# Group means one projection later, a copy ahead of a root, and norm chunks later in two feed-forward tails

## The chip, the cores and the metric

The kernel runs on one NeuronCore of one Trainium2 chip. The time is the device time of one execution in microseconds (us); lower is better. Times of a kernel are given as the median of several executions. A profile is one execution recorded by the hardware profiler; its rows give what each engine did from the start of its span. The engines are PE (TensorE: matmuls; PEld is its weight load), DVE (VectorE), ACT (ScalarE), POOL (GpSimd) and SP (SyncE, which here only issues transfers).

## The reference

One decoder block on a sequence of 1024 tokens of width 1024, in float32:

```python
x = x + 0.5*gt1 * swiglu(modulate(rmsnorm(x, g_ffn1), sh1, sc1), w1, w3, w2)      # feed-forward 1, 2816 wide
h = modulate(rmsnorm(x, g_mix), sh2, sc2)
x = x + gt2 * hybrid_mixer(h, ...)
x = x + 0.5*gt3 * swiglu(modulate(rmsnorm(x, g_ffn2), sh3, sc3), ...)             # feed-forward 2
return modulate(rmsnorm(x, g_final), shf, scf)

# hybrid_mixer, the convolution half (512 channels, 8 groups of 64):
y = gate_b * causal_short_conv(gate_c * u, conv_w)        # three taps
y = rmsnorm(y by group of 64) * conv_norm_g
# the attention half: 4 heads of differential attention; both halves share one output projection
```

The shifts, scales and gates come from a conditioning vector through `w_ada`.

## The kernel before

Everything is held transposed: channels on the 128 partitions, tokens along the free axis, in two halves of 512. Each fp32 operand is split into a high and a low part (`Mh`/`Ml` for the mixer's weights, `Hh`/`Hl` for its input, `Wh`/`Wl` in the feed-forwards), and a product is three matmuls: high by high, high by low, low by high. ACT writes the high part by a copy; DVE subtracts it from the source for the low part. Every engine's instructions are written out by hand in order, and semaphores (`wait_ge`) join them. An instruction that waits holds up all that is behind it on its engine.

**The mixer's convolution half** runs in two groups, `cg` 0 and 1. A group has 12 projections L = 0 to 11, each 24 matmuls of 128x512 into one of six banks: q = L // 3 counts the pairs (tile, half), tile 0 being q 0 and 1, tile 1 being q 2 and 3, and L % 3 chooses u, C or B. The weights of a tile are three units: units 0 to 2 serve L0 to L5, units 3 to 5 serve L6 to L11 (numbers within the first group), so L6 is the first reader of unit 3, L7 of unit 4, L8 of unit 5. PE waits for the low part of a unit (`lo_done`, line 1713) only at even q. After the projections come 16 output tiles t (L = 12 + t), which DVE adds to `X` (`add_out`, line 1256). The group's L0 to L4 run in `project_new`, which takes the input's chunks as they arrive (`h_ready`).

For each q a small chain normalises the tile: DVE multiplies C by u into `CU` (1312), applies the taps (1317, 1321), multiplies by B (1326); ACT squares (794); PE takes the mean over each group of channels (`group_mean(q)`: four small matmuls); ACT takes the root (798 before); DVE inverts and spreads it (1332, 1334); PE broadcasts it (`group_bcast(q)`); DVE scales the tile into `TmpG` (1339); ACT and DVE split that (`g_hi`, `g_lo`). `MEANS[cg]` and `BCASTS[cg]` name the L after which mean and broadcast stand in PE's order.

The splits of the weights stand inside this chain. On ACT, unit 3's high part (`split_hi`, line 709) follows root 0, and unit 4's follows `g_hi` of q 0, hence broadcast 0. On DVE, unit 3's low part (`split_lo`, line 1180) follows the spread of root 0, and unit 4's follows `g_lo` of q 0 and the `CU` of q 1. `copy_u(q)` (781) is ACT's copy of the projection u out of its bank.

**The feed-forward's down part** is seven products of 11 steps g. In the last one (i = 6) PE turns the loop: steps 7 to 10 run for output tile 0, then for tile 1, and so on (`TURNED`). Meanwhile the other half's norm is already applied: DVE's `norm_mul` (1243), ACT's `norm_chunk` (741, two copies in the first feed-forward, one in the second) and, in the first feed-forward only, DVE's `norm_lo` (1249), chunk by chunk. `BEHIND` names which chunk (c0 to c7) and which of the output additions (x0 to x2) stands behind which step g on ACT and DVE. `down_hi` and `down_lo`, which prepare the operands, stand ahead of them in each step. Behind the first feed-forward PE consumes the chunks at once; behind the second they go to the output.

Of the kernel before, what the change touches and what calls it, by code (L numbers as in the profile page):

```python
# [117 lines left out]

TURN = NG - 4
TURNED = [(d, g) for d in (0, 1) for g in (7, 8, 9)] + [(0, 10), (1, 10)] + [(d, g) for d in (2, 3) for g in (7, 8, 9, 10)]  # L120
BEHIND = {6: ("c0",), 7: ("c1", "c2"), 8: ("c3", "c4"), 9: ("c5", "x0"), 10: ("c6", "x1", "c7", "x2")}

X_AFTER = (8, 14, 25, 52)

# [14 lines left out]
    _at += _n  # L139
NCOLS = _at  # L140

MEANS, BCASTS = ((4, 6, 9), (3, 6, 9)), ((5, 7, 10), (4, 7, 10))


def conv_bank(cg, L):
    return (L + (0 if cg else 4)) % BANKS


def program(nc, up_w, down_w, units, ada, x_t, cols_d, lam_d, rope_d, square_d, out_t):
    ctx = ExitStack()  # L150
    with ctx:
# [116 lines left out]
        def half(h):  # L268
            return slice(h * HALF, (h + 1) * HALF)

        def blk(b):
            return slice(b * P, (b + 1) * P)
# [12 lines left out]
        def unit(n):  # L285


            if n < U_Q1:
                return Mh[:, n % RING, :], Ml[:, n % RING, :]
            if n < U_WO + 2:  # L290
                return tuple(m[:, 1 + (n - U_Q1) % 2, :] for m in (Mh, Ml))
            return Wo[:, n - U_WO - 2, 0, :], Wo[:, n - U_WO - 2, 1, :]
# [17 lines left out]
        def sem(name):  # L310
            sems[name] = ctx.enter_context(nc.semaphore(name))
            return sems[name]
# [43 lines left out]
        evac, aevac, ghi, g_ready = sem("evac"), sem("aevac"), sem("ghi"), sem("g_ready")  # L356
# [205 lines left out]
        def _(act):  # L562
# [106 lines left out]
            def down(ph):  # L669
                q = 2 + 4 * ph  # L670
                for m in range(N_DOWN):
# [11 lines left out]
                    if ph == 0 and i == 6 and g in (4, 5, 8):  # L683
                        split_first((4, 5, 8).index(g))
                    for what in BEHIND.get(g, ()) if i == 6 else ():
                        if what[0] == "c":
# [12 lines left out]
            def split_first(n):  # L699

                act.wait_ge(gt_lo, 6 * NG + 2 * n + 2)
                act.wait_ge(raw_loaded[n], 16)
                nc.scalar.activation(Mh[:, n, :], Mr[:, n, :], ACT.Copy).then_inc(hi_done, 1)

            def split_hi(n, wait, value):

                act.wait_ge(wait, value)
                act.wait_ge(raw_loaded[n % RING], 16 * (n // RING + 1))
                nc.scalar.activation(unit(n)[0], Mr[:, n % RING, :], ACT.Copy).then_inc(hi_done, 1)  # L709

            def g_hi(slot, h, wait, value):
                act.wait_ge(wait, value)
                nc.scalar.activation(Gh[:, slot, half(h)], TmpG[:, h, :], ACT.Copy).then_inc(ghi, 1)
# [60 lines left out]
            for cg in range(2):  # L774
                J, E, n0 = JOBS["conv"] + 28 * cg, EVAC["conv"] + 24 * cg, U_CONV + 8 * cg

                def copy_u(q):
                    act.wait_ge(job_done, J + 3 * q + 1)
                    if q >= 2:
                        act.wait_ge(evac, E + 2 * q - 3)  # L780
                    nc.scalar.activation(TmpA[:, q % 2, :], PS[:, conv_bank(cg, 3 * q), :], ACT.Copy).then_inc(aevac, 1)

                if cg:
                    for c in (1, 2):
                        split_hi(n0 + c, job_done, J)
                else:
                    act.wait_ge(hh_done, NH * KT)
                copy_u(0)
                for q in range(4):
                    jt, h, cq = q // 2, q % 2, 4 * cg + q  # L790
                    if h == 1:
                        split_hi(n0 + 3 * jt + 4, job_done, J + 3 * q + 2)
                    act.wait_ge(evac, E + 2 * q + 2)
                    nc.scalar.activation(Sq[:, h, :], CT[:, half(h)], ACT.Square).then_inc(csq_done, 1)
                    if h == 1:
                        split_hi(n0 + 3 * jt + 5, job_done, J + 3 * q + 3)
                    act.wait_ge(cmean_done, cq + 1)
                    nc.scalar.activation(Root[:, 0:8], PS[:, 6, 0:8], ACT.Sqrt, bias=EpsC[:, 0:1])\
                        .then_inc(croot_done, 1)
                    if q < 3:  # L800
                        copy_u(q + 1)
                    if h == 0:
                        split_hi(n0 + 3 * jt + 3, job_done, J + 3 * q + 4)
                    g_hi(jt, h, cg_done, cq + 1)
# [135 lines left out]
        def _(dve):  # L940
# [190 lines left out]
            def down(ph):  # L1131
                q = 2 + 4 * ph
                for m in range(N_DOWN):
# [14 lines left out]
                    if ph == 0 and i == 6 and g in (5, 6, 9):  # L1148
                        split_lo((5, 6, 9).index(g))
                    for what in BEHIND.get(g, ()) if i == 6 else ():  # L1150
                        n = int(what[1])
# [24 lines left out]
            def split_lo(n):  # L1176

                dve.wait_ge(hi_done, n + 1)
                hi, lo = unit(n)
                nc.vector.tensor_tensor(lo, Mr[:, n % RING, :], hi.bitcast(F32), ALU.subtract).then_inc(lo_done, 1)  # L1180
# [260 lines left out]
        def _(pe):  # L1441
            def mm(out, lhs, rhs, first, last):
                return nc.tensor.matmul(out, lhs, rhs, start=first, stop=last)  # L1443
# [160 lines left out]
            def project_new(first, n, h, units):  # L1604


                for k in range(KT + LAG * (units - 1)):
                    for w in range(units):
                        if not w * LAG <= k < KT + w * LAG:
                            continue  # L1610
                        if w == 0:
                            pe.wait_ge(h_ready, KT * h + k + 1)
                        if k == w * LAG:
                            pe.wait_ge(lo_done, n + w + 1)
                            pe.wait_ge(x_added, 28 if h else (24, 24, 25)[w])
                        products(conv_bank(0, first + w), n + w, h, (k - w * LAG,))
                    if h == 0 and k == KT - 1:
                        mean(3)
                    if h == 0 and k == KT + 1:
                        bcast(3)  # L1620
# [59 lines left out]
            for cg in range(2):  # L1680
                J, E, A, G = JOBS["conv"] + 28 * cg, EVAC["conv"] + 24 * cg, AEVAC["conv"] + 4 * cg, GDONE["conv"] + 4 * cg
                n0 = U_CONV + 8 * cg

                def evicted(L):
                    q, w = L // 3, L % 3
                    if L >= 12:
                        return evac, E + 8 + L - 12 + 1
                    return (evac, E + 2 * q + w) if w else (aevac, A + q + 1)

                def group_mean(q):  # L1690
                    pe.wait_ge(csq_done, 4 * cg + q + 1)
                    for b in range(4):
                        made = mm(PS[:, 6, 2 * b:2 * b + 2], Sq[:, q % 2, blk(b)], MeanG[:], True, True)
                    made.then_inc(cmean_done, 1)

                def group_bcast(q):
                    pe.wait_ge(cspread_done, 4 * cg + q + 1)
                    for b in range(4):
                        made = mm(PS[:, 7, blk(b)], Spread[:, q % 2, blk(b)], ident, True, True)
                    made.then_inc(cbc_done, 1)  # L1700

                for L in range(12):
                    q, w = L // 3, L % 3
                    if cg == 0 and L < 5:
                        if w == 0:
                            project_new(L, n0, q, 2 if q else 3)
                    else:
                        if L >= BANKS:
                            pe.wait_ge(*evicted(L - BANKS))
                        elif cg:  # L1710
                            pe.wait_ge(evac, E)
                        if q % 2 == 0:
                            pe.wait_ge(lo_done, n0 + 3 * (q // 2) + w + 1)
                        project(conv_bank(cg, L), n0 + 3 * (q // 2) + w, q % 2)
                    if L in MEANS[cg]:
                        group_mean(MEANS[cg].index(L))
                    if L in BCASTS[cg]:
                        group_bcast(BCASTS[cg].index(L))
                pe.wait_ge(lo_done, n0 + 8)
                for t in range(NH * KT):  # L1720
                    pe.wait_ge(*evicted(12 + t - BANKS))
                    if t % KT == 0:
                        pe.wait_ge(g_ready, G + 3 + t // KT)
                    out_job(conv_bank(cg, 12 + t), (n0 + 6, n0 + 7), [(Gh[:, f, :], Gl[:, f, :]) for f in range(GF)], t)
                    if t == 0:
                        group_mean(3)
                    if t == 3:
                        group_bcast(3)
# [240 lines left out]
```

## Time and profile before

| | |
|---|---|
| median of 3 runs | 1923.37 us (1922.18 to 1923.48) |
| the profiled execution's own time | 1920.22 us |
| its span | 1918.4 us |
| PE busy | 1837.8 us, 96% of the span |
| DVE busy | 1265.1 us, 66% |
| ACT busy | 780.6 us, 41% |
| POOL busy | 262.0 us, 14% |
| chain that ended last | PE 85%, DVE 7%, ACT 4%, issue 2% |

PE's busy share counts its pipelined matmuls as they overlap, so 96% is not PE at its peak. What matters for a change of order are the places where PE stands idle, and what it waits for there: the table of waits and the timeline. A start-to-start distance of about 0.23 us between two 128x512 matmuls is an unhindered PE at full clock. In a timeline row the brackets at the end give the engine's idle time before the instruction and what ended it.

### The profile page before, as it was taken

How to read it: one execution, taken by the hardware profiler on the slowest of the kernel's cores; microseconds unless marked ns; L12 is line 12 of the kernel's file. 1: busy time of each engine (PE TensorE's matmuls, PEld its weight loads, DVE VectorE, ACT ScalarE, POOL GpSimd, SP SyncE). 2: the span in 40 equal slices, each digit the busy share in tenths (PEclk: the TensorE clock that was granted, in tenths of full speed). 3: DMA queues.
4: the chain of work that ended last, by engine and by line, in shares of the span. 5: the costliest groups of instructions: out<-in, count | busy, mean ns of one | idle time of the engine just before them, and what ended most of it. 6: DMA issues, size and time to landing. Idle time of an engine off the chain costs nothing.

```text
span 1918.4 us, 22914 instructions
## 1 busy us (share of the span) xinstructions
PE 1837.8 (96%) x8248; PEld 1471.3 (77%) x8248; DVE 1265.1 (66%) x1946; ACT 780.6 (41%) x1401; POOL 262.0 (14%) x404
## 2 busy tenths in 40 slices
PE   5999999999999999999999999799999999999997
PEld 2778888888788877888876666677888888878885
DVE  5777777777476776434226668787666766567767
ACT  4633333333344555111126565563333333344445
POOL 2021121211210000000303330001111211111000
PEclk9999999999999999999999999899999999999998
DMA  8166565665775312111201110415454554487432
GB/s 314 55 209 218 183 228 187 206 228 176 252 216 158 100 62 76 44 45 44 77 28 39 44 34 1 176 44 198 149 197 154 190 188 149 157 265 218 128 99 88
DMA packets 99984, 269.76 MB, mean 141 GB/s; under 512 B 13088, under 2 KB 13472, under 8 KB 99744
## 3 DMA queue, kind: packets, MB, share of 16 engines
q1 hardware_dynamic: 62064, 146.30, 22.2%
q0 software_dynamic: 34304, 117.46, 18.2%
q10 hardware_dynamic: 3504, 4.53, 1.0%
q8 instruction: 66, 1.08, 0.2%
q14 instruction: 46, 0.38, 0.1%
HBM read 209.53 MB, written 54.53 MB: 138 GB/s over the span
## 4 chain that ended last, share of the span: by engine, by line
PE 85%; DVE 7%; ACT 4%; issue 2%; ACTq 1%; DMA 1%; POOL 0%; DVEq 0%; POOLq 0%
PE PS L1447 60%; PE PS L1443 24%; ACTq L819 1%; PE PS L1848 1%; ACT PR L841 1%; DVE TmpA L1243 0%; DVE NMax L1356 0%; DVE X L1256 0%; DMA X<-x_t 0%; DVE Wl L987 0%; DVE AdaSum L1202 0%; DVE Wl L984 0%; DVE SqSum L1225 0%; DVE CT L1321 0%; ACT Mh L709 0%
## 5 line engine op out<-in xcount | busy, mean ns | idle before, releaser
L1447 PE MATMUL PS<-Bh,Wh 128*128 128x512 f32 x1120 | 442.6, 395 | 5.5 <-ACT T L618 5.5
L1447 PE MATMUL PS<-Bl,Wh 128*128 128x512 f32 x1120 | 441.9, 395 | 0.0
L1447 PE MATMUL PS<-Bh,Wl 128*128 128x512 f32 x1120 | 441.3, 394 | 0.0
L1447 PEld LDWEIGHTS PS<-Bh,Wh 128*128 128x128 f32 x1120 | 210.6, 188 | 57.5 <-DVE Wl L952 6.3
L1447 PEld LDWEIGHTS PS<-Bh,Wl 128*128 128x128 f32 x1120 | 210.5, 188 | 50.3
L1447 PEld LDWEIGHTS PS<-Bl,Wh 128*128 128x128 f32 x1120 | 210.6, 188 | 49.1
L1447 PE MATMUL PS<-Wh 128*128 128x512 f32 x616 | 240.3, 390 | 3.4 <-DVE Wl L987 1.7
L1447 PE MATMUL PS<-Wl,Wh 128*128 128x512 f32 x616 | 239.7, 389 | 0.0
L1447 PE MATMUL PS<-Wh,Wl 128*128 128x512 f32 x616 | 239.7, 389 | 0.0
L984 DVE TENSOR_TENSOR Wl<-RawB,Wh 128x512 fp32r<-128x512 f32 x154 | 106.6, 692 | 136.4 <-ACT Wh L593 135.3
L593 ACT ACTIVATE Wh<-RawB 128x512 fp32r<-128x512 f32 x154 | 97.3, 632 | 230.1 <-PE PS L1447 230.1
L618 ACT ACTIVATE T<-PS 128x512 f32<-128x512 f32 x120 | 71.8, 598 | 265.4 <-PE PS L1447 265.4
L952 DVE TENSOR_TENSOR Wl<-Sums,Wh 128x512 fp32r<-128x512 f32 x160 | 110.3, 690 | 90.5 <-ACT Wh L583 90.3
L1447 PEld LDWEIGHTS PS<-Wh 128*128 128x128 f32 x616 | 115.6, 188 | 28.3 <-DVE T L1018 2.5
L952 DVE TENSOR_TENSOR Wl<-Raw,Wh 128x512 fp32r<-128x512 f32 x136 | 92.9, 689 | 66.0 <-ACT Wh L583 65.8
L1447 PEld LDWEIGHTS PS<-Wh,Wl 128*128 128x128 f32 x616 | 115.6, 188 | 24.2
L1447 PEld LDWEIGHTS PS<-Wl,Wh 128*128 128x128 f32 x616 | 115.6, 188 | 23.8
L1443 PE MATMUL PS<-Hh,Mh 128*128 128x512 f32 x320 | 130.8, 409 | 2.1 <-DVE Hl L1249 1.3
L583 ACT ACTIVATE Wh<-Sums 128x512 fp32r<-128x512 f32 x160 | 98.2, 623 | 79.5 <-DVE Sums L970 54.8
L1443 PE MATMUL PS<-Hl,Mh 128*128 128x512 f32 x320 | 126.5, 395 | 0.0
L1443 PE MATMUL PS<-Hh,Ml 128*128 128x512 f32 x320 | 126.0, 394 | 0.0
L1008 DVE TENSOR_TENSOR T<-T,PS 128x512 f32<-128x512 f32 x120 | 82.3, 686 | 45.9 <-PE PS L1447 43.3
(184 smaller groups left out, 2875.4 us busy)
## 6 DMA issues: line engine op xcount, KB each, us to landing
Raw<-up_w SPq DMA_DIRECT2D x88, 512.0 KB, 5.5
Ada<-ada POOLq DMA_DIRECT2D x72, 512.0 KB, 4.4
g_dram<-T SPq DMA_DIRECT2D x88, 256.0 KB, 2.2
W2s<-down_w POOLq DMA_DIRECT2D x88, 256.0 KB, 4.5
s_dram<-W2s POOLq DMA_DIRECT2D x88, 256.0 KB, 2.5
GQ<-g_dram POOLq DMA_DIRECT2D x88, 256.0 KB, 3.5
RawB<-s_dram SPq DMA_DIRECT2D x88, 256.0 KB, 2.8
RawB<-down_w SPq DMA_DIRECT2D x66, 256.0 KB, 2.7
```

The lines of the kernel that those rows point to most:

```text
L583: nc.scalar.activation(Wh[:, slot, :], src, ACT.Copy).then_inc(w_hi, 1)
L593: nc.scalar.activation(Wh[:, 4 + m % 4, :], RawB[:, m % 8, :], ACT.Copy).then_inc(w_hi, 1)
L618: nc.scalar.activation(T[:, 4 * w + q, :], PS[:, x + (j == 1), :], ACT.Copy).then_inc(acopy, 1)
L819: act.dma_start(to[a:a + 32, :], TmpA[a ^ 32:(a ^ 32) + 32, slot, :]).then_inc(shifted[j % 2], 16)
L841: nc.scalar.activation(PR[:, c, 0:P * (i + 1)], scores(c, 0, i + 1), ACT.Exp, bias=NMax[:, c:c + 1], accum_out=Sum[:, c:c + 1]).then_inc(e ...
L952: nc.vector.tensor_tensor(Wl[:, slot, :], src, Wh[:, slot, :].bitcast(F32), ALU.subtract).then_inc(w_lo, 1)
L984: nc.vector.tensor_tensor(Wl[:, 4 + m % 4, :], RawB[:, m % 8, :], Wh[:, 4 + m % 4, :].bitcast(F32), ALU.subtract).then_inc(w_lo, 1)
L1008: nc.vector.tensor_tensor(T[:, 4 * w + q, :], T[:, 4 * w + q, :], PS[:, x + (j != 4), :], ALU.add)\
L1443: return nc.tensor.matmul(out, lhs, rhs, start=first, stop=last)
L1447: return nc.tensor.matmul(out, lhs, rhs, start=first, stop=last, skip_group_check=True)
L1848: made = nc.tensor.transpose(PS[:, 4 + r, blk(b % 4)], PR[:, 2, blk(b)], ident)
```

## The change

Four edits. In the first convolution group the means of q 0 and q 1 stand behind L5 and L7 instead of L4 and L6, and their broadcasts behind L6 and L8 instead of L5 and L7. On ACT, `copy_u(q + 1)` stands ahead of the root of q instead of behind it, in both groups. L0 of the second group waits for the last but one output tile of the first group, not the last (its bank was used by tile 14). In both feed-forwards' last product the chunks stand later in `BEHIND`.

```diff
-BEHIND = {6: ("c0",), 7: ("c1", "c2"), 8: ("c3", "c4"), 9: ("c5", "x0"), 10: ("c6", "x1", "c7", "x2")}
+BEHIND = {6: ("c0",), 7: ("c1",), 8: ("c2", "c3"), 9: ("c4", "x0"), 10: ("c5", "x1", "c6", "x2", "c7")}
...
-MEANS, BCASTS = ((4, 6, 9), (3, 6, 9)), ((5, 7, 10), (4, 7, 10))
+MEANS, BCASTS = ((5, 7, 9), (3, 6, 9)), ((6, 8, 10), (4, 7, 10))
...
                     if h == 1:
                         split_hi(n0 + 3 * jt + 5, job_done, J + 3 * q + 3)
+                    if q < 3:
+                        copy_u(q + 1)
                     act.wait_ge(cmean_done, cq + 1)
                     nc.scalar.activation(Root[:, 0:8], PS[:, 6, 0:8], ACT.Sqrt, bias=EpsC[:, 0:1])\
                         .then_inc(croot_done, 1)
-                    if q < 3:
-                        copy_u(q + 1)
                     if h == 0:
                         split_hi(n0 + 3 * jt + 3, job_done, J + 3 * q + 4)
...
                         elif cg:
-                            pe.wait_ge(evac, E)
+                            pe.wait_ge(evac, E if L else E - 1)
```

On PE, at the end of L5 in the first group, this stood there before (`Square,Spread` is the broadcast of q 0, `Hh_91` the input of the first half, so the row that waits is the first of L6):

```order
 L1443 MATMUL PS<-Hh_92,Ml 128x512
 L1443 MATMUL PS<-Square,Spread 128x128 [waits cspread_done]
 L1443 MATMUL PS<-Square,Spread 128x128 x3
 L1443 MATMUL PS<-Hh_91,Mh 128x512 [waits lo_done,aevac]
 L1443 MATMUL PS<-Hl_93,Mh 128x512
```

and this stands there now (`MeanG,Sq` is the mean of q 0):

```order
 L1443 MATMUL PS<-Hh_92,Ml 128x512
 L1443 MATMUL PS<-MeanG,Sq 128x2 [waits csq_done]
 L1443 MATMUL PS<-MeanG,Sq 128x2 x3
 L1443 MATMUL PS<-Hh_91,Mh 128x512 [waits lo_done,aevac]
 L1443 MATMUL PS<-Hl_93,Mh 128x512
```

The mean of q 0 came a projection (24 matmuls) ahead of L6 and now comes directly ahead of it; at the end of L6, in the same way, the broadcast of q 0 now stands directly ahead of L7.

On ACT, the same stretch from the first `copy_u` on; `Mh` are the high parts of units 3, 4 and 5:

```order
 L781 ACTIVATE TmpA<-PS 128x512
 L794 ACTIVATE Sq<-CT 128x512
-L798 ACTIVATE Root<-PS,EpsC 128x8
 L781 ACTIVATE TmpA<-PS 128x512
+L800 ACTIVATE Root<-PS,EpsC 128x8
 L709 ACTIVATE Mh<-Mr 128x1024
 L713 ACTIVATE Gh<-TmpG 128x512
```

The copy moved from behind the root to ahead of it; unit 3's high part still stands behind the root, and unit 4's behind `Gh`.

On DVE, in the first feed-forward's last product, from chunk 4's multiplication (`TmpA<-X,PS`) on, as it stood before (`Hl_93` is a chunk's low part, `X<-PS,Gate,X` an output addition):

```order
 L1243 TENSOR_TENSOR TmpA<-X,PS 128x512
 L1249 TENSOR_TENSOR Hl_93<-TmpG,Hh_91 128x512
 L1180 TENSOR_TENSOR Ml<-Mr,Mh 128x1024
 L1243 TENSOR_TENSOR TmpA<-X,PS 128x512
 L1249 TENSOR_TENSOR Hl_93<-TmpG,Hh_91 128x512
 L1127 SCALAR_TENSOR_TENSOR X<-PS,Gate,X 128x512
 L1243 TENSOR_TENSOR TmpA<-X,PS 128x512
```

and as it stands now from chunk 3's multiplication on:

```order
 L1243 TENSOR_TENSOR TmpA<-X,PS 128x512
 L1249 TENSOR_TENSOR Hl_93<-TmpG,Hh_91 128x512
 L1180 TENSOR_TENSOR Ml<-Mr,Mh 128x1024
 L1243 TENSOR_TENSOR TmpA<-X,PS 128x512
 L1249 TENSOR_TENSOR Hl_93<-TmpG,Hh_91 128x512
 L1127 SCALAR_TENSOR_TENSOR X<-PS,Gate,X 128x512
 L1243 TENSOR_TENSOR TmpA<-X,PS 128x512
```

The rows read alike, and what moved is the chunk: one pair fewer stands ahead of the weight's `Ml` and ahead of each output addition, so every chunk from the second on comes one place later against them. POOL's and SP's orders are the same in both kernels.

## Rows read from the trace of the kernel before

**Rows 1.** who waited for whom, PE, 684 to 960 us: total, times, longest

```profile
PE PS L1443 <- ACT Sq L794: 3.4, 4, 1.9
```

**Rows 2.** timeline, PE: start, duration, instruction, count [idle before it, releaser]

```profile
750.76 1.05 PE L1443 MATMUL PS<-MeanG,Sq 128*128 128x2 f32 x8 [0.58 <-ACT Sq L794]
751.67 0.48 PE L1443 MATMUL PS<-Hh,Mh 128*128 128x512 f32 x1
...
757.26 1.06 PE L1443 MATMUL PS<-Square,Spread 128*128 128x128 f32 x8
...
765.71 1.05 PE L1443 MATMUL PS<-MeanG,Sq 128*128 128x2 f32 x8 [1.86 <-ACT Sq L794]
766.62 0.48 PE L1443 MATMUL PS<-Hh,Mh 128*128 128x512 f32 x1
...
772.25 1.05 PE L1443 MATMUL PS<-Square,Spread 128*128 128x128 f32 x8
```

**Rows 3.** timeline, ACT, the first root and what follows it

```profile
751.85 0.27 ACT L798 ACTIVATE Root<-PS,EpsC 128x8 f32<-128x8 f32 x1 [1.14 <-PE PS L1443]
752.01 0.59 ACT L781 ACTIVATE TmpA<-PS 128x512 f32<-128x512 f32 x1
752.49 1.06 ACT L709 ACTIVATE Mh<-Mr 128x1024 fp32r<-128x1024 f32 x1
```

**Rows 4.** timeline, DVE, the low parts of units 3 and 4

```profile
753.58 1.23 DVE L1180 TENSOR_TENSOR Ml<-Mr,Mh 128x1024 fp32r<-128x1024 f32 x1 [0.77 <-ACT Mh L709]
...
761.01 1.22 DVE L1180 TENSOR_TENSOR Ml<-Mr,Mh 128x1024 fp32r<-128x1024 f32 x1
```

**Rows 5.** timeline, DVE, first tap of q 0 and of q 2

```profile
747.71 1.54 DVE L1321 SCALAR_TENSOR_TENSOR CT<-CU,Cols,CT 128x512 f32<-128x512 f32 x2
...
776.63 0.75 DVE L1321 SCALAR_TENSOR_TENSOR CT<-CU,Cols,CT 128x512 f32<-128x512 f32 x1
```

**Rows 6.** busy time by stretch, all engines, then granted clock, DMA share, GB/s

```profile
106.00:111.00 5.00, 4.73 (x14) 3.77 (x15) 4.23 (x8) 1.89 (x5) 1.08 (x2) 0.66 0.84 286
1297.00:1302.00 5.00, 4.91 (x15) 3.91 (x16) 4.00 (x7) 1.88 (x4) 1.08 (x2) 0.66 0.81 286
762.00:770.00 8.00, 6.13 (x32) 4.84 (x31) 4.58 (x8) 2.33 (x4) 0.00 (x0) 1.00 0.34 109
```

**Rows 7.** timeline, PE, the wait ahead of the first of these stretches

```profile
106.27 0.47 PE L1447 MATMUL PS<-Bh,Wh 128*128 128x512 f32 x1 [2.74 <-ACT T L618]
```

**Rows 8.** timeline, DVE and PE, end of the first group

```profile
820.80 0.75 DVE L1256 SCALAR_TENSOR_TENSOR X<-PS,Gate,X 128x512 f32<-128x512 f32 x1 [0.62 <-PE PS L1443]
...
822.98 0.50 PE L1443 MATMUL PS<-Hh,Mh 128*128 128x512 f32 x1 [0.84 <-DVE X L1256]
```

**Rows 9.** timeline, ACT, the third weight's high part and chunk 3

```profile
714.46 1.04 ACT L703 ACTIVATE Mh<-Mr 128x1024 fp32r<-128x1024 f32 x1
715.40 0.80 ACT L741 ACTIVATE TmpG<-TmpA,Mod,Scale 128x512 f32<-128x512 f32 x1
```

**Rows 10.** timeline, DVE, chunks behind the first feed-forward's last product

```profile
717.55 1.22 DVE L1180 TENSOR_TENSOR Ml<-Mr,Mh 128x1024 fp32r<-128x1024 f32 x1
718.69 0.68 DVE L1243 TENSOR_TENSOR TmpA<-X,PS 128x512 f32<-128x512 f32 x1
...
719.89 0.74 DVE L1127 SCALAR_TENSOR_TENSOR X<-PS,Gate,X 128x512 f32<-128x512 f32 x1
720.55 0.68 DVE L1243 TENSOR_TENSOR TmpA<-X,PS 128x512 f32<-128x512 f32 x1
...
723.60 0.69 DVE L1249 TENSOR_TENSOR Hl<-TmpG,Hh 128x512 fp32r<-128x512 f32 x1
```

**Rows 11.** timeline, PE, the first matmul on chunk 6

```profile
724.35 0.50 PE L1443 MATMUL PS<-Hh,Mh 128*128 128x512 f32 x1
```

**Rows 12.** timeline, PE and DVE, end of the second feed-forward

```profile
1901.17 0.39 PE L1447 MATMUL PS<-Wh,Wl 128*128 128x512 f32 x1
...
1901.89 0.74 DVE L1127 SCALAR_TENSOR_TENSOR X<-PS,Gate,X 128x512 f32<-128x512 f32 x1
```

## The prediction, made before the changed kernel ran

> **What bounds the kernel now.** The shares in the table say PE, and the chain of waits runs through it for 85%, so an edit counts only where it changes PE's idle time. I read three views. The table of waits for the stretch of the convolution gives PE's waits on the squares: four, 3.4 us in all [rows 1]. PE's timeline shows where they stand: 0.58 idle ahead of mean 0 and 1.86 ahead of mean 1, while the broadcasts at 757.26 and 772.25 wait for nothing [rows 2]. Then ACT's and DVE's timelines show what is queued behind the mean's root, and that is the view that decides.
>
> Two distances are used throughout. A projection is 5.59 us where it follows a mean or a broadcast (751.67 to 757.26) and 24 x 0.229 = 5.50 elsewhere; the small group between projections takes 0.91 if it was waited for (765.71 to 766.62) and 0.81 if not [rows 2]. An unhindered PE would start mean 0 0.75 us earlier (0.58 idle, and the last matmul's overlap with its successor), at 750.01.
>
> **First edit, means and broadcasts later.** L5 needs neither mean nor new weights, so it starts at 750.01 and ends at 755.51; its square is long done, so mean 0 stands there without a wait, and the 0.75 is gone. But L6 is next, and it is the first reader of unit 3. In before, root 0 starts 1.09 after the mean (750.76 to 751.85), the copy 0.16 later, unit 3's high part at 752.49, and its low part from 753.58 to 754.81 [rows 3, 4]. L6 began after 758.08, so it had 3.3 us in hand. Now the root starts at about 755.51 + 0.98 = 756.49 (a mean not waited for saves 0.1), the high part 0.16 behind it, since the copy is out of the way (second edit: 0.48 saved), and the low part 1.09 later: 757.74 to 758.97. PE, ready at 756.32, can start L6 at about 759.04: a new wait of 2.7 us. All that is behind L6 waits with it.
>
> L6 ends at 764.63 and broadcast 0 follows. L7 is the first reader of unit 4, whose high part is behind `g_hi` of q 0 on ACT and whose low part is behind `g_lo` and `CU` on DVE, all after broadcast 0. In before the broadcast starts at 757.26 and the low part ends at 761.01 + 1.22 = 762.23, 4.97 later [rows 2, 4]; L7 came at 766.62. Now L7 is ready 0.81 after the broadcast's start and can begin at 764.63 + 4.97 + 0.05 = 769.65: a second new wait, 4.2 us. The projection that used to stand between broadcast and reader was the cover.
>
> L7 ends at 775.24. Mean 1 would be ready 765.71 - 757.26 = 8.45 after broadcast 0, at 773.08, so its 1.86 wait (2.03 of PE's time) is gone. Unit 5 is split ahead of root 1, so L8 starts on time at 776.05 and broadcast 1 at 781.64. L9 ends at 788.04. Mean 2, unmoved, now has one projection between it and broadcast 1, not two: the first tap of q 2 runs 776.63 - 772.25 = 4.38 after broadcast 1, and from first tap to mean are 3.05 (747.71 to 750.76) [rows 2, 5], together 7.43, so it starts at 789.07: a third wait, 1.0. Then 0.91, L10 and broadcast 2 at 795.57. In before this is at 772.25 + 0.81 + 5.50 + 5.59 + 0.81 + 5.59 = 790.55. The first edit costs 5.0 us. Behind broadcast 2 nothing changes: the weights behind it are split as before, and SP's later loads of units 6 to 8, released by the low parts of 3 to 5, still have more than 15 us.
>
> Bounds: if the root chain is as tight as in the best case and unit 3 comes half a microsecond sooner, 4.5; if every hand-over costs a tenth more, 5.5.
>
> **The granted clock.** [...] Around the 1.86 wait it stayed at 1.00 [rows 6]. [...] I take 1.7 for each, 3.4 us; bounds are 0 and 3.6. L6 and L7 stretch by it, and the next chain starts only at their ends, so nothing absorbs it.
>
> [...]
>
> **Second edit, the copy ahead of the root.** The copy waits for a projection that is done by the mean's start in all cases, and its 0.59 fits into the 1.0 between that and the root. In the first group its gain is in the sum above; elsewhere no weight is waited for: 0. If it delayed a root, the broadcast behind has a projection of cover.
>
> **Third edit.** L0 of the second group starts at 822.98 after 0.84 idle for tile 15's addition; tile 14's ends at 820.80 + 0.75 = 821.55 [rows 8], before PE's 821.97. Gain 1.0. L1 still waits for tile 15, 5.5 later, and finds it done.
>
> **Fourth edit, first feed-forward.** PE's first projections take the chunks one by one. In before chunk 6's low part starts at 723.60, ends at 724.29, and its first matmul starts at 724.35 [rows 10, 11], 0.15 late: no slack. Now, between the weight's `Ml` and chunk 6, DVE has four instructions more (a multiplication, a low part, x2 and its square sum): 3 x 0.60 + 0.66 = 2.46 by the pitches [rows 10]. Against that, `Ml` itself can start a chunk earlier, since ACT reaches it one chunk sooner: ACT's high part is over by 715.40 [rows 9] less two copies of 0.71, and `Ml` moves from 717.55 to about 716.1. Net 2.46 - 1.42 = 1.0 late on chunk 6, all of it PE's. Chunk 7 has enough time. The root and mean behind were not waited for, so x2's earlier end buys nothing. Cost 1.0, bounds 0 (if ACT's queue lets DVE run tighter) and 1.5.
>
> **Fourth edit, second feed-forward.** The last addition x3 starts at 1901.89, while PE's last matmul is over at 1901.17 + 0.39 = 1901.56 [rows 12]; DVE was late by some 0.25. With chunk 7 moved behind x2 the count of instructions ahead is the same, but a short wait for ACT goes. Gain 0.2, bounds 0.3 and -0.7 (c7 in front of ACT's last square).
>
> **Sum.** 5.0 + 3.4 - 1.0 + 1.0 - 0.2 = +8.2 us against the profiled execution's 1920.22 (span 1918.4 and 1.8 around it), thus 1928.4. The median of before is 3.15 above that execution, and a median is what will be compared: 1923.37 + 8.2, rounded, 1931.5.
>
> **Rivals.**
>
> *The waits come, the clock does not fall twice.* One fall: +6.5, 1929.9; none: +4.8, 1928.2. [...]
>
> *The means' waits are simply removed.* If the two low parts were in time after all, PE would lose 0.75 + 2.03 + 1.0 + 0.2 of idle and gain the 1.0 of chunk 6: -3.0, or -4.0 without chunk 6: 1920.4 to 1919.4, the end on the other side. Its point is the low part of unit 4: with less than 0.8 us between broadcast 0 and it, this decides. Against it stands 4.97 in the trace, in a queue that the edit leaves in the same order. [...]
>
> *Only unit 4 is late.* If unit 3's split were covered: 8.2 - 2.7 - 1.7 = +3.8, 1927.2. Against it: the root must start before the split.
>
> *More than counted.* A third fall, or a fall displaced in the attention that follows: +10, 1933.4.
>
> **How the numbers follow.** Two falls 0.5; one or none 0.3; only unit 4 late 0.07; more 0.08; removed waits 0.05. The range for 8 in 10 is 1926.5 to 1933.5: it takes in no fall with a lower median, and up to the last case. What a measurement of this kernel can tell from no change is 0.2%, 3.8 us. The first two cases and "more" are slower; half of "only unit 4" is within, and the removed waits are half within, half faster. With a margin for a cover that I overlook: faster 0.04, same 0.08, slower 0.88.
>
> **What would show it.** In the profile of the changed kernel: no idle ahead of the first two means; PE waiting for `Ml` (L1180) about 2.3 and 3.8 as the brackets count it, ahead of L6 and L7; 0.6 ahead of mean 2; the granted clock at 0.5 for some 3 us behind each; L0 of the second group without a wait; a wait of about 1 for `Hl` (L1249) near 724. The forecast is wrong if `Ml` is in none of PE's waits.

## The result and the profile after

| | before | changed |
|---|---|---|
| median | 1922.36 us (6 runs, 1920.48 to 1923.48) | 1929.74 us (6 runs, 1926.98 to 1935.08) |
| ratio | | 1.0039, 95% interval 1.0026 to 1.0051 |
| profiled execution, own time | 1920.22 us | 1935.08 us |
| its span | 1918.4 us | 1933.3 us |

The change makes the kernel slower by 0.39%, 7.5 us (5.0 to 9.8). The profiled execution is the slowest of the six, 14.9 us above before's profiled one; 6 of these lie in a stretch that the change does not touch (the fourth row of the table of distances).

PE's waits from 684 to 960 us of the changed kernel: what was waited for, total, times, longest.

```profile
PE PS L1443 <- DVE Ml L1180: 6.7, 2, 4.0
PE PS L1443 <- DVE Hl L1249: 2.1, 4, 0.8
PE PS L1443 <- ACT Sq L794: 1.8, 3, 0.8
```

The waits for squares, 3.4 in [rows 1], have shrunk to 1.8, and 6.7 for `Ml`, the low part of a weight unit, have taken their place. PE's timeline of the first group, as in [rows 2]:

```profile
757.83 0.95 PE L1443 MATMUL PS<-MeanG,Sq 128*128 128x2 f32 x8
761.44 0.47 PE L1443 MATMUL PS<-Hh,Mh 128*128 128x512 f32 x1 [2.65 <-DVE Ml L1180]
...
767.04 1.05 PE L1443 MATMUL PS<-Square,Spread 128*128 128x128 f32 x8
772.14 0.76 PE L1443 MATMUL PS<-Hh,Mh 128*128 128x512 f32 x1 [4.05 <-DVE Ml L1180]
...
779.99 0.95 PE L1443 MATMUL PS<-MeanG,Sq 128*128 128x2 f32 x8
...
793.82 1.05 PE L1443 MATMUL PS<-MeanG,Sq 128*128 128x2 f32 x8 [0.85 <-ACT Sq L794]
```

Mean 0 (757.83) has no idle ahead of it. L6 follows at 761.44 after 2.65 for `Ml`. Broadcast 0 is at 767.04, L7 at 772.14 after 4.05 for `Ml`. Mean 1 (779.99) waits for nothing, mean 2 (793.82) 0.85 for its squares. The rows on ACT and DVE that answer to [rows 3, 4], ACT's first:

```profile
752.91 0.58 ACT L781 ACTIVATE TmpA<-PS 128x512 f32<-128x512 f32 x1
758.82 0.27 ACT L800 ACTIVATE Root<-PS,EpsC 128x8 f32<-128x8 f32 x1 [5.33 <-PE PS L1443]
758.99 1.05 ACT L709 ACTIVATE Mh<-Mr 128x1024 fp32r<-128x1024 f32 x1
768.90 0.63 ACT L713 ACTIVATE Gh<-TmpG 128x512 fp32r<-128x512 f32 x1 [8.87 <-DVE TmpG L1339]
769.44 1.04 ACT L709 ACTIVATE Mh<-Mr 128x1024 fp32r<-128x1024 f32 x1
```

```profile
760.07 1.22 DVE L1180 TENSOR_TENSOR Ml<-Mr,Mh 128x1024 fp32r<-128x1024 f32 x1 [0.28 <-ACT Mh L709]
...
769.57 0.69 DVE L1184 TENSOR_TENSOR Gl<-TmpG,Gh 128x512 fp32r<-128x512 f32 x1 [0.69 <-ACT Gh L713]
770.17 0.68 DVE L1312 TENSOR_TENSOR CU<-TmpA,PS 128x512 f32<-128x512 f32 x1
770.77 1.22 DVE L1180 TENSOR_TENSOR Ml<-Mr,Mh 128x1024 fp32r<-128x1024 f32 x1
```

On ACT the copy stands at 752.91, out of the way; the root at 758.82 waited for mean 0, and the high parts of units 3 and 4 start 0.17 behind the root and 0.54 behind `Gh`. On DVE the low parts follow: 760.07, and 770.77 as the fourth instruction behind broadcast 0. L6 and L7 start as these end (761.29 and 771.99). The queues' order is the old one; only the cover has gone.

The other edits: chunk 6's first matmul with its wait (726.66; 0.15 late in [rows 11]), L0 of the second group (831.79; 0.84 of idle in [rows 8]) behind its predecessor, and the last mean (1918.58):

```profile
726.66 0.51 PE L1443 MATMUL PS<-Hh,Mh 128*128 128x512 f32 x1 [0.78 <-DVE Hl L1249]
...
831.57 0.39 PE L1443 MATMUL PS<-Gh,Ml 128*128 128x512 f32 x1
831.79 0.39 PE L1443 MATMUL PS<-Hh,Mh 128*128 128x512 f32 x1
...
1918.58 1.05 PE L1443 MATMUL PS<-Mean,SqSum 128*128 128x1 f32 x8 [2.29 <-DVE SqSum L1225]
```

The wait ahead of L0 is gone, its start lies 0.22 behind its predecessor's. The last mean waits 2.29; in before its row is

```profile
1904.08 1.05 PE L1443 MATMUL PS<-Mean,SqSum 128*128 128x1 f32 x8 [2.52 <-DVE SqSum L1225]
```

Distances between marks that every profile has, in us (profiled executions; "changed, again" is a second profile of the changed kernel, from the first experiment):

| stretch | before | changed | changed, again | forecast of the difference |
|---|---|---|---|---|
| mean behind i = 6, g = 2 to second half's mean (4th edit) | 38.99 | 40.02 (+1.03) | 40.03 (+1.04) | +1.0 |
| to mean 0 of the first group | 22.15 | 26.90 (+4.75) | 26.90 (+4.75) | +4.75 |
| to mean 0 of the second group | 94.35 | 95.94 (+1.59) | 96.61 (+2.26) | -0.75, and +3.4 for the clock |
| from broadcast 3 of the second group to the second feed-forward's tail mean | 973.17 | 979.24 (+6.07) | 975.60 (+2.43) | 0 |
| to the last mean | 29.12 | 28.86 (-0.26) | 28.89 (-0.23) | -0.2 |

Between the third row's end and the fourth row's start lie 56.7 us in all three executions. Of the 14.9 us, 1.3 lie ahead of the first mark and 0.4 behind the last.

The stretch of 973 us is the one to be careful with. Between 984 and 1235 us lies the attention, where the granted clock falls and rises again, three to six times in each of the thirteen profiled executions:

```profile
984.00:1222.00 238.00, 217.34 (x1114) 160.69 (x1113) 157.46 (x287) 132.34 (x325) 54.17 (x36) 0.97 0.14 42
```

(the attention of before) and of the changed kernel

```profile
985.00:1235.00 250.00, 228.24 (x1140) 169.49 (x1139) 158.00 (x286) 133.80 (x328) 54.16 (x36) 0.95 0.13 41
```

The clock's share of full speed lost is 0.03 x 238 = 7 us in the one and 0.05 x 250 = 12.5 in the other. Read microsecond by microsecond, it is 0.50 for 3.4 us or twice that in each fall, so 1.7 us of full speed or twice that are lost; before's execution has four such steps of 1.7 there, the changed one seven. The three more are 5.1 of the 6.07 us.

### The profile page after: what moved, and what is told of

Same layout as the page of the kernel before. It is cut to its first block, busy times and chain, and to the rows that moved or that the text cites. A ratio compares the mean times of both kernels' runs of the same rounds, so it can differ in the third digit from the quotient of the medians.

```text
span 1933.3 us, 22914 instructions
## 1 busy us (share of the span) xinstructions
PE 1845.2 (95%) x8248; PEld 1477.1 (76%) x8248; DVE 1265.2 (65%) x1946; ACT 781.1 (40%) x1401; POOL 262.0 (14%) x404
## 4 chain that ended last, share of the span: by engine, by line
PE 84%; DVE 7%; ACT 4%; issue 2%; ACTq 1%; DMA 1%; POOL 0%; SPq 0%; DVEq 0%; POOLq 0%
PE PS L1447 59%; PE PS L1443 24%; ACTq L819 1%; ACT PR L841 1%; PE PS L1848 1%; DVE TmpA L1243 1%; DVE NMax L1356 0%; DMA X<-x_t 0%; DVE Ml L1180 0%; DVE SqSum L1225 0%; DVE X L1127 0%; DVE Wl L987 0%; DVE X L1256 0%; DVE Wl L984 0%; DMA Raw<-up_w 0%
```

## The experiments

All comparisons are with the kernel before, run on the same chip beside them.

**The changed kernel again**

> The changed kernel once more, for another profiled execution. Theory A: +7 to +8 us over before; from the mean of the first feed-forward's tail to the first mean of the second group +7 us (the three waits and the clock), the last mean 0.26 sooner, and the 6 us that the first profiled execution lost between the groups and the second feed-forward's tail are not there again, or are another number of steps of 1.7 (the clock's falls in the attention). Rival (the change also slows the attention): the 6 us are there again.

1929.79 us, 1.0035 (1.0022 to 1.0049). The stretch with the attention is +2.43 this time, not +6.07; over the five profiles with mean 0 in its old place it varies from 971.52 to 975.90 us, over the eight with mean 0 a projection later from 971.04 to 979.24. The two longest, 979.24 and 978.79, are both of the latter, so these single profiles alone do not rule the rival out. The executions as a whole speak against it: the mean granted clock, which is given for each of them, makes 33.9 us of full speed lost in the five executions of the changed kernel and 30.9 in the ten of before beside them, 3.0 more (an estimate, as the clock is given to 0.001, 1.9 us). The two steps in the first group (3.4) fill that, and nothing is left for the attention. The median, which is what was forecast, does not carry the first execution's 6 us: the four other stretches sum to +7.1 and +7.8, the medians say +7.5.

The two profiles differ at L6. PE's stretch of 10 us around it in the first and in the second execution:

```profile
758.00:768.00 10.00, 7.35 (x40) 6.17 (x39) 1.85 (x3) 1.21 (x2) 0.00 (x0) 1.00 0.17 54
```

```profile
757.00:767.00 10.00, 7.75 (x29) 6.30 (x30) 1.79 (x3) 0.84 (x1) 0.00 (x0) 0.83 0.17 54
```

The same wait (2.65 and 2.66) left the clock at 1.00 in the one and cost a fall in the other. PE's rows of the second execution, where L6 lasts 7.20 and L7 6.92 instead of 5.59:

```profile
759.25 0.47 PE L1443 MATMUL PS<-Hh,Mh 128*128 128x512 f32 x1 [2.66 <-DVE Ml L1180]
...
766.45 1.05 PE L1443 MATMUL PS<-Square,Spread 128*128 128x128 f32 x8
771.56 0.77 PE L1443 MATMUL PS<-Hh,Mh 128*128 128x512 f32 x1 [4.05 <-DVE Ml L1180]
...
778.48 0.95 PE L1443 MATMUL PS<-MeanG,Sq 128*128 128x2 f32 x8
```

**The means alone**

```diff
-MEANS, BCASTS = ((4, 6, 9), (3, 6, 9)), ((5, 7, 10), (4, 7, 10))
+MEANS, BCASTS = ((5, 7, 9), (3, 6, 9)), ((6, 8, 10), (4, 7, 10))
```

> Only the first group's means and broadcasts stand a projection later; the rest is as before. Theory A (weights queued behind the chain): PE waits for Ml ahead of L6 (about 3.1, since the copy is still between root and split) and ahead of L7 (about 4.0), 0.6 to 0.9 ahead of mean 2, and the low clock behind the wait of L7: +7.5 us over before, between +6 and +9. Rival B (the slowdown comes from the chunks or from the attention's clock, the means only lose their waits): -2.8 us, no wait for Ml.

1933.30 us, 1.0061 (1.0047 to 1.0075), +11.7: theory A's direction, beyond its range. The waits are as said:

```profile
759.45 0.77 PE L1443 MATMUL PS<-Hh,Mh 128*128 128x512 f32 x1 [3.14 <-DVE Ml L1180]
...
767.72 1.05 PE L1443 MATMUL PS<-Square,Spread 128*128 128x128 f32 x8
772.82 0.76 PE L1443 MATMUL PS<-Hh,Mh 128*128 128x512 f32 x1 [4.05 <-DVE Ml L1180]
...
781.26 0.95 PE L1443 MATMUL PS<-MeanG,Sq 128*128 128x2 f32 x8
```

What was mis-sized is the clock. L6 lasts 767.72 - 759.45 = 8.27 and L7 781.26 - 772.82 = 8.44, where 5.59 is full speed: 5.5 us for two falls, and each takes in two steps of 1.7 (part of it in the wait itself). The sum without the clock, 5.0 + 0.5 for the copy that still stands between root and split, and these 5.5 give 11.0.

**Everything but the means**

```diff
-MEANS, BCASTS = ((5, 7, 9), (3, 6, 9)), ((6, 8, 10), (4, 7, 10))
+MEANS, BCASTS = ((4, 6, 9), (3, 6, 9)), ((5, 7, 10), (4, 7, 10))
```

> The changed kernel with the means and broadcasts where they were before; copy, tile wait and chunks stay changed. Theory A: -0.2 us against before (-1.0 for L0 of the second group, +1.0 for chunk 6, -0.2 in the tail), so no difference that can be measured. Rival B: +4 us or more.

1922.53 us, 1.0003 (0.9995 to 1.0011). Rival B's +4 is excluded: with the experiment before it, the slowdown is in the means' move, as theory A has it.

**The chunks alone**

```diff
-BEHIND = {6: ("c0",), 7: ("c1", "c2"), 8: ("c3", "c4"), 9: ("c5", "x0"), 10: ("c6", "x1", "c7", "x2")}
+BEHIND = {6: ("c0",), 7: ("c1",), 8: ("c2", "c3"), 9: ("c4", "x0"), 10: ("c5", "x1", "c6", "x2", "c7")}
```

> Only the chunks' places in the last down steps are changed. Theory A: +0.8 us: a wait of about 0.8 (as the brackets count it) for Hl of chunk 6 behind the first feed-forward, 0.25 less wait for the last mean at the end. Rival C (later chunks cost nothing since x2 and the last square come sooner): 0 or below, no wait for Hl before the mean of the second half.

1922.78 us, 1.0005 (0.9997 to 1.0014): too small for the timing, but the marks have it: +1.04 in the first stretch, -0.24 in the last. In the second-half mean's stretch PE waits 0.8 for `Hl`.

**Tile wait and copy alone**

```diff
-                            pe.wait_ge(evac, E)
+                            pe.wait_ge(evac, E if L else E - 1)
...
+                    if q < 3:
+                        copy_u(q + 1)
                     act.wait_ge(cmean_done, cq + 1)
...
-                    if q < 3:
-                        copy_u(q + 1)
```

> Only the copy ahead of the root and the weaker wait of L0 of the second group. Both theories: -1.0 us, all from the 0.84 of idle ahead of L0 that goes; the copy's move changes no wait of PE.

1921.46 us, 0.9998 (0.9985 to 1.0012), inconclusive as a time. From mean 0 to mean 0 of the second group it is -1.17 us, and PE's waits for squares stay at 3.4.

**Unit 3 split ahead of root 0** (on the changed kernel; DVE's `split_lo(n0 + 3)` moves likewise ahead of the wait for `croot_done`)

```diff
+                    if q == 0 and not cg:
+                        split_hi(n0 + 3, job_done, J + 4)
                     act.wait_ge(cmean_done, cq + 1)
...
-                    if h == 0:
+                    if h == 0 and (q or cg):
                         split_hi(n0 + 3 * jt + 3, job_done, J + 3 * q + 4)
```

> The changed kernel, but unit 3 of the first group is split ahead of root 0 on ACT and on DVE. Theory A (PE waits because the split is queued behind the chain): the wait for Ml ahead of L6 (2.65 in the changed kernel's brackets) is gone, the one ahead of L7 (4.05) stays: 2.7 us less than the changed kernel's +7.5, so about +4.7 over before, +3 to +6 by how often the clock falls. Rival (the wait is for something else that comes with the later mean, such as the bank or the raw weight): +7.5, both waits stay.

1926.63 us, 1.0022 (1.0013 to 1.0032), +4.2, in the range named. One wait for `Ml` is left:

```profile
PE PS L1447 <- DVE Ml L1182: 4.1, 1, 4.1
PE PS L1447 <- DVE Hl L1251: 2.1, 4, 0.8
PE PS L1447 <- ACT Sq L794: 1.8, 3, 0.9
```

**Unit 4 split ahead of broadcast 0 as well, and alone** (`split_hi(n0 + 4, job_done, J + 5)` ahead of `g_hi` of q 0, `split_lo(n0 + 4)` ahead of the wait for `cbc_done`)

> The changed kernel, but units 3 and 4 are split ahead of root 0 and of broadcast 0. Theory A: no wait for Ml at all; about 0.6 to 0.85 of idle in the brackets ahead of mean 1 and of mean 2; -1 us against before by the sum (-2.8 for the old waits, +2.1 for these two, +1.0 chunk 6, -1.0 L0, -0.2 tail), down to -2.5 where the clock falls less often. Rival: +4 or more.

> The changed kernel, but only unit 4 is split ahead of broadcast 0. Theory A: the wait ahead of L6 stays at 2.65, the one ahead of L7 is gone, about 0.6 to 0.85 ahead of means 1 and 2: +1.6 us over before without a fall of the clock at L6, +4 with one. Rival: +7.5.

Both: 1924.09 us, 1.0008 (0.9999 to 1.0017), +1.5. Unit 4 alone: 1928.14 us, 1.0030 (1.0020 to 1.0040), +5.8. The waits ahead of L6 and L7 go and stay as theory A says, but "no wait for Ml at all" is wrong, and with both moved the forecast of -1 is missed by 2.5. With both moved, PE shows this ahead of mean 1 and of L8:

```profile
770.28 1.05 PE L1451 MATMUL PS<-MeanG,Sq 128*128 128x2 f32 x8 [0.85 <-ACT Sq L794]
772.58 0.77 PE L1451 MATMUL PS<-Hh,Mh 128*128 128x512 f32 x1 [1.24 <-DVE Ml L1184]
```

The second row is the third unit: unit 5's high part is behind the square of q 1 on ACT, and once L7 is on time, L8 comes 1.5 us too early for it. That is 1.5 of the 2.5; in the profiled execution, the slowest of the eleven, the clock fell behind it as well (0.50 for 6.8 us from 771.9), and its stretches without the attention's sum to +3.2. I had called unit 5 in time, which holds only behind the 4.2 that L7 waits. Unit 4 alone is above its +1.6 to +4. The stretches of its profiled execution, the attention's left out, sum to 1.03 + 4.75 - 0.83 - 0.26 = +4.7: the +1.6, 1.5 for this third wait, and the clock's fall at L6 (0.50 from 760.7 to 764.1). The profiled execution is the fastest of the eight by 3.8 us. What is between +4.7 and +5.8 stays open.

**Other places for the means**

```diff
-MEANS, BCASTS = ((5, 7, 9), (3, 6, 9)), ((6, 8, 10), (4, 7, 10))
+MEANS, BCASTS = ((4, 7, 9), (3, 6, 9)), ((5, 8, 10), (4, 7, 10))
```

> Means of the first group behind L4, L7 and L9 and broadcasts behind L5, L8 and L10, so that each reader of a new unit keeps a projection between it and what its split waits for; tile wait and copy as changed; chunks later only in the second feed-forward. Theory A: the wait of 1.86 ahead of mean 1 is gone, 0.85 comes ahead of mean 2, L0 waits for nothing: -2.2 us against before, and up to -1.7 more for the falls of the clock that the 1.86 wait brings in some executions. Rival (the waits move and add up to the same): 0.

1920.33 us, 0.9992 (0.9983 to 1.0001), -1.5: as a time not told from no change. Its profile is in line with theory A by its waits (0.55 ahead of mean 0, none ahead of mean 1, 0.85 ahead of mean 2) and by its stretches (-2.16 from mean 0 to mean 0 of the second group, -0.24 at the end), where the rival has 0.

**The chain ahead of the scaling**

```diff
+                    tile_of(0)
+                    split_lo(n0 + 3)
+                    tile_of(1)          # CU, taps and B of q 1; unit 4's low part inside
+                    invert(0)
+                    split_lo(n0 + 5)
+                    scaled(0)
+                    invert(1)
+                    tile_of(2)
+                    scaled(1)
...
-                    if t == 0:
+                    if t == 1:
                         group_mean(3)
```

(ACT's order follows: both high parts and the square of q 1 stand ahead of root 0.)

> Means and broadcasts of the first group as changed, but there units 3, 4 and 5 are split ahead of what PE takes between them, and the convolution of q 1 and q 2 is worked out ahead of the scaling of q 0 and q 1, so that no mean waits for a broadcast; in both groups mean 3 stands behind output tile 1; tile wait and copy as changed, chunks later only in the second feed-forward. Theory A (what PE waits for is only the place in ACT's and DVE's queues): no wait of PE in the first group but at most 0.1; -2.8 - 1.3 - 1.0 - 0.2 = -5.3 us against before. Rival (DVE becomes the bound once the work is pulled together): waits for squares or Ml of 1 to 2 us remain, -2 to -3.

1916.31 us, 0.9961 (0.9949 to 0.9974): 7.5 us below before (5.0 to 9.8), and 13.5 below the changed kernel's median of the same session. It is faster than both. Of PE's waits from 684 to 960 us none is left in the chain; the remaining ones all stand ahead of mean 0:

```profile
PE PS L1508 <- DVE Wl L1020: 1.7, 1, 1.7
PE PS L1504 <- DVE Hl L1282: 1.3, 3, 0.5
PE PS L1504 <- DVE X L1160: 0.4, 1, 0.4
```

From mean 0 to mean 0 of the second group it is 9.61 shorter, against +4.78 ahead of it (L5 now stands before mean 0), together -4.8. With -0.7 behind it (mean 3 of the second group) and -0.2 at the end that makes -5.7, where -5.3 was expected. The rest up to -7.5 can be the clock: by the mean granted clock the five executions lose 29.1 us of full speed and the ten of before 30.9, 1.8 less (an estimate, as above). Before's wait of 1.86 was followed by a fall in two of the four profiles that have it, and here it is gone. The rival falls: DVE had the room. Which of the edits (the splits, the convolution ahead of the scaling, mean 3) brought how much inside the first group was not taken apart.

**Chunk 0 behind the last down operands, too**

```diff
-BEHIND = ({6: ("c0",), 7: ("c1", "c2"), 8: ("c3", "c4"), 9: ("c5", "x0"), 10: ("c6", "x1", "c7", "x2")},
+BEHIND = ({7: ("c0", "c1"), 8: ("c2", "c3"), 9: ("c4", "c5", "x0"), 10: ("c6", "c7", "x1", "x2")},
```

> As v2_chain_ahead, and behind the first feed-forward's last product chunk 0 stands behind the last down operands, not ahead of them (places 7: c0 c1, 8: c2 c3, 9: c4 c5 x0, 10: c6 c7 x1 x2). Theory A: PE's wait of 1.74 for Wl (L987) goes, 1.9 us with the overlap, perhaps 0.5 of it given back to the mean of the second half: -6.7 us against before. Rival (the chunks come too late): a new wait for Hl takes its place, -5.3 or less.

1916.03 us, 0.9961 (0.9948 to 0.9973): as a time no faster than the one before it, where 1.4 was forecast. The wait of 1.74 for `Wl` is gone, a wait of 0.77 for a chunk's `Hl` at 724.95 has come, and the stretch is 0.81 shorter instead of 1.9. Both theories have a part; a time cannot tell 0.8 us.

**The clock over all profiles.** One profiled execution each (two of the changed kernel); what the granted clock did behind the wait, in brackets the time at 0.50:

| PE's wait (brackets) | fell | did not |
|---|---|---|
| 1.86 ahead of mean 1 | everything but the means (3.4); the chunks alone (3.4) | before; tile wait and copy alone |
| 0.85 ahead of mean 1 and 1.24 ahead of L8 | both units early (6.8) | unit 4 early |
| 2.65 ahead of L6 | changed, again (3.4); unit 4 early (3.4) | changed |
| 3.14 ahead of L6 | the means alone (6.8) | |
| 4.05 ahead of L7 | changed (6.8); changed, again (3.4); the means alone (6.8); unit 3 early (3.4) | |

The wait of 1.74 for `Wl` near 711 is in twelve profiles, and behind it the clock fell in none: it is 1.00 from 700 to 750 in all of them.

## Why the prediction came out

The mechanism and most of its terms were right, and the time (1931.5 forecast, 1929.74 measured) is inside the range. Point by point:

- **Wait ahead of L6**, 2.7 from ACT's and DVE's queue: measured 3.61 - 0.81 = 2.8 between mean 0 and L6. Shown to be the queue by the unit 3 experiment.
- **Wait ahead of L7**, 4.2: measured 772.14 - 767.04 - 0.81 = 4.3. Shown by moving unit 4.
- **Wait ahead of mean 2**, 1.0: measured 1.24 - 0.23 = 1.0.
- **The clock**, 3.4 as two falls of 1.7: this term was mis-sized. The 1.7 is 0.34 x 5 by the two stretches at 0.66 in [rows 6]; as a fixed cost behind each new wait no run shows it. On PE's path the falls were 2.3 in one execution (L7 alone, 779.99 - 772.14 = 7.85 against 5.59) and 2.9 in the other (L6 1.6, L7 1.3). Behind the first wait (2.65) the clock fell in one of these two executions, not in the other, which the prediction had as its first rival, and a fall was one step of 1.7 or two, which it had not: with the means alone moved, two waits of 3.14 and 4.05 cost 5.5, beyond the 3.6 that it gave as the most. That the term came out near its size is in part luck. What decides whether the clock falls behind a wait is not shown: it means 1.00 and 0.83 over 10 us around the same wait of 2.65. The measured +7.5 lies between the forecast's case (+8.2) and that rival's (+6.5).
- **Third edit**, -1.0: shown by its idle of 0.84 that is gone, and -1.17 together with the copy's move; no run has it alone.
- **Fourth edit**, +1.0 and -0.2: +1.03 and -0.26.
- **Second edit**, 0.5 and nothing elsewhere: with the copy behind the root L6 waited 3.14 instead of 2.65. That those 0.5 us also made the double fall in the means-alone runs more likely is argued, not shown.
- Wrong in passing: "unit 5 is split ahead of root 1, so L8 starts on time" is true of the changed kernel but rests on L7's wait, and I did not see it until the waits were taken away.

The base was a choice as well: the profile's execution plus 8.2 would have given 1928.4, the median plus 8.2 gave 1931.5; the measured one lies between, since the median of before was 1.0 lower in the later runs.

## What to carry to other kernels

Before an instruction that others are queued behind is moved later, list what stands behind it on every engine of its chain and who reads that first: here the means lost 2.8 us of wait and the weight splits behind their roots brought 7.1. If a wait is to go, split the queue, so that what does not depend on the chain stands ahead of it; that, with mean 3 and the tile wait moved too, gave 7.5 us where moving the waiter lost as much. Price a wait on a busy TensorE with its clock as well: here that of 1.86 us was followed by a fall in two profiles of four, that of 4.05 in all four, at 1.3 to 2.9 us a fall.

## What the runs showed of the hardware

The granted clock fell in steps. From 680 us to the attention's end it is 0.50 for 3.4 or 6.8 us in each fall of the thirteen profiles, so each loses 1.7 or 3.4 us of full speed, nothing between. A part of a fall can lie in the idle time itself: behind the wait of 4.05 in the changed kernel the clock means 0.66 over 10 us, 3.4 lost, and L7 is 2.3 longer.

```profile
768.00:778.00 10.00, 5.95 (x17) 4.64 (x17) 6.98 (x9) 3.64 (x5) 0.00 (x0) 0.66 0.16 52
```

Two of PE's waits in before are 2.74 long, that of [rows 7] and

```profile
1297.09 0.47 PE L1447 MATMUL PS<-Bh,Wh 128*128 128x512 f32 x1 [2.74 <-ACT T L618]
```

and the clock means 0.66 over 5 us behind each [rows 6].

The same wait of 2.65 in the same kernel was followed by a fall in one execution and by none in the other (0.83 and 1.00 over 10 us), and the wait of 1.86, in kernels that differ only elsewhere, by a fall in two profiles of four. In the two profiled executions of the changed kernel the spans differ by 5.3 us (1933.3 and 1928.0), and 3.6 of it lies in the stretch with the attention (979.24 and 975.60), where no instruction differs.
